# Opening of a two-layer decoder trunk: a first weight unit in two halves, other load orders, another order of TensorE's first steps

## The reference

```python
h = rms_norm(x, norm1_g[l])        # x * rsqrt(mean(x*x) + 1e-6) * g
proj = h @ w_in[l]                 # 1024 -> D_IN columns
...                                # three token mixers, gates, merge
x = x + merged @ w_out[l]
h2 = rms_norm(x, norm2_g[l])
x = x + jnp.square(jax.nn.relu(h2 @ w_ff1[l])) @ w_ff2[l]
```

## Time and profile before

| | us |
|---|---|
| Median of 3 runs (1759.27 to 1759.74) | 1759.31 |
| Span of the profiled execution, first to last instruction | 1757.8 |
| Its own time less its span, taken as median less span | about 1.5 |
| PE busy | 1743.5 (99%) |
| POOL busy | 1067.3 (61%) |
| DVE busy | 957.3 (54%) |
| ACT busy | 690.3 (39%) |

### The profile page before, as it was taken

One profiled execution on the slowest core, in us unless ns is written; L12 is line 12 of the kernel. 1 busy time (PEld: TensorE's weight loads), 2 busy tenths in 40 slices (PEclk: granted clock), 3 DMA queues, 4 the chain that ended last, 5 costly groups with the idle time before them and its releaser, 6 DMA issues.

```text
span 1757.8 us, 26298 instructions
## 1 busy us (share of the span) xinstructions
PE 1743.5 (99%) x10006; PEld 1427.0 (81%) x10006; DVE 957.3 (54%) x1565; ACT 690.3 (39%) x1241; POOL 1067.3 (61%) x572
## 2 busy tenths in 40 slices
PE   8999999999999999999999999999999999999999
PEld 7787888778888888888787888887888888888887
DVE  6796626653442555444566965366443435444445
ACT  6423316550104444444355243176411154444442
POOL 7454466246665777777774535662456657777776
PEclk9999999999999999999999999999999999999999
DMA  6222133133235666666442221331322356666655
GB/s 201 84 73 73 50 96 108 37 98 94 88 101 163 161 173 157 167 168 157 130 156 80 77 62 61 96 96 37 115 89 92 100 153 159 162 173 157 170 153 144
DMA packets 58896, 207.18 MB, mean 118 GB/s; under 512 B 6368, under 2 KB 8704, under 8 KB 58784
## 3 DMA queue, kind: packets, MB, share of 16 engines
q1 hardware_dynamic: 47520, 164.94, 30.0%
q0 software_dynamic: 9216, 33.56, 10.2%
q10 hardware_dynamic: 2048, 7.10, 1.1%
HBM read 184.61 MB, written 4.19 MB: 107 GB/s over the span
## 4 chain that ended last, share of the span: by engine, by line
PE 97%; ACT 1%; DVE 1%; issue 0%; DMA 0%; POOL 0%; SPq 0%; DVEq 0%; ACTq 0%; POOLq 0%
PE ps L666 23%; PE ps L668 22%; PE ps L667 22%; PE ps L1263 6%; PE ps L1265 6%; PE ps L1264 6%; PE ps L1135 2%; PE ps L1144 1%; PE ps L1157 1%; PE ps L685 1%; PE ps L908 1%; PE ps L895 0%; PE ps L945 0%; PE ps L1207 0%; PE ps L931 0%
## 5 line engine op out<-in xcount | busy, mean ns | idle before, releaser
L666 PE MATMUL ps<-hHi,wHi 128*128 128x512 f32 x1360 | 552.9, 407 | 0.0
L668 PE MATMUL ps<-hHi,wLo 128*128 128x512 f32 x1360 | 530.4, 390 | 0.0
L667 PE MATMUL ps<-hLo,wHi 128*128 128x512 f32 x1360 | 529.8, 390 | 0.0
L566 POOL TENSOR_SCALAR wHi<-wraw 128x1024 fp32r<-128x1024 f32 x168 | 181.8, 1082 | 491.6 <-PE ps L668 474.4
L571 POOL TENSOR_TENSOR wLo<-wraw,wHi 128x1024 fp32r<-128x1024 f32 x168 | 415.9, 2476 | 13.8
L597 POOL TENSOR_TENSOR wLo<-w,wHi 128x1024 fp32r<-128x1024 f32 x96 | 239.2, 2514 | 140.5 <-ACT wHi L1694 140.1
L666 PEld LDWEIGHTS ps<-hHi,wHi 128*128 128x128 f32 x1360 | 255.4, 188 | 59.1 <-issue 7.0
L667 PEld LDWEIGHTS ps<-hLo,wHi 128*128 128x128 f32 x1360 | 255.7, 188 | 54.7 <-issue 3.8
L668 PEld LDWEIGHTS ps<-hHi,wLo 128*128 128x128 f32 x1360 | 255.3, 188 | 54.2
L1263 PE MATMUL ps<-wHi,fHi 128*128 128x512 f32 x448 | 174.8, 390 | 1.7 <-issue 1.7
L1265 PE MATMUL ps<-wHi,fLo 128*128 128x512 f32 x448 | 174.4, 389 | 0.0
(11 more groups left out here) (337 smaller groups left out, 2674.7 us busy)
## 6 DMA issues: line engine op xcount, KB each, us to landing
wraw<-stream SPq DMA_DIRECT2D x224, 512.0 KB, 3.5
w<-stream SPq DMA_DIRECT2D x64, 512.0 KB, 4.3
w<-w POOLq DMA_DIRECT2D x32, 512.0 KB, 6.8
b<-stream SPq DMA_DIRECT2D x16, 512.0 KB, 3.5
b<-stream POOLq DMA_DIRECT2D x16, 512.0 KB, 6.1
w<-stream POOLq DMA_DIRECT2D x16, 512.0 KB, 8.1
xin<-x SPq DMA_DIRECT2D x4, 512.0 KB, 6.3
y<-x ACTq DMA_DIRECT2D x1, 2048.0 KB, 10.2
```

The costliest lines, as they stand in the source:

```text
L566: nc.gpsimd.tensor_scalar(wHi[:, slot], wraw[:, slot % RAW], 1.0, 0.0, ALU.mult, ALU.add).then_inc(unit_high, 1)
L666: mm(o, lh[lc], rh[rc], start=start, stop=False)
L667: mm(o, lh[lc], rl[rc], start=False, stop=False)
L668: return mm(o, ll[lc], rh[rc], start=False, stop=stop)
```

## The change

SP's order of loads becomes: x part 0, first half of weight unit 0, x part 1, second half of unit 0, unit 1, x parts 2 and 3, tables. POOL's order becomes: high and low of unit 0's first half, high of its second half, high of unit 1, low of unit 0's second half, low of unit 1. ACT's queue loads the first eight columns of the parameters (norm1's factors) first, then the identity, then the other parameters. PE's hand-written order becomes another, the first pass of a `high_step` waits for `h_high` instead of `h_lo`, and `sum_stream` has all of unit 0 and four low steps of unit 1 ahead of it and four behind it. PE now waits at its start for the identity and the norm factors both. Two pairs of semaphores are made one each (`const_zero` and `tri_done`; `lanes_zero` and `lanes_set`), with their waits at the count that fits.

```diff
             for part in range(4):
-                cols = np.s_[part * 256:(part + 1) * 256]
-                sp.dma_start(xin[:, :, cols], ...).then_inc(x_in[part], 16)
-                if part == 1:
-                    for slot in range(RAW):
-                        load_unit(slot, slot)
+            def load_half(half, loaded):
+                cols = np.s_[half * 512:(half + 1) * 512]
+                sp.dma_start(wraw[:, 0, cols], stream[0][:, cols]).then_inc(loaded, 16)
+            load_x(0)
+            load_half(0, first_loaded)
+            load_x(1)
+            load_half(1, raw_loaded[0])
+            load_unit(1, 1)
+            for part in range(2, 4):
+                load_x(part)
...
-            for slot in range(RAW):
-                high(slot, 1)
-            for slot in range(RAW):
-                low(slot, slot)
+            high_half(0, first_loaded, first_halves)
+            low_half(0, first_halves, FIRST_HIGH, first_halves)
+            high_half(1, raw_loaded[0], unit_high)
+            high(1, 1)
+            low_half(1, unit_high, 1, unit_split)
+            low(1, 1)
...
-            pe.wait_ge(ident_in, 16)
+            pe.wait_ge(ident_in, 32)
...
                 def high_step(slot, k):
-                    pe.wait_ge(unit_high, slot + 1)
-                    pe.wait_ge(h_lo, k + 1)
+                    if slot == 0 and k < KD // 2:
+                        pe.wait_ge(first_halves, FIRST_HIGH)
+                    else:
+                        pe.wait_ge(unit_high, slot + 1)
+                    pe.wait_ge(h_high, k + 1)
                     mm(bank_of(slot), wHi[...], hHi[:, k], ...)
+                    pe.wait_ge(h_lo, k + 1)
                     mm(bank_of(slot), wHi[...], hLo[:, k], ...)
...
                 if layer == 0:
-                    turn_stream(0, range(0, 4))
+                    turn_stream(0, range(0, 2))
                     high_step(0, 0)
+                    turn_stream(0, range(2, 4))
                     high_step(0, 1)
-                    turn_stream(0, range(4, 6))
                     high_step(1, 0)
                     high_step(1, 1)
+                    low_step(0, 0)
+                    low_step(0, 1)
                     high_step(0, 2)
+                    high_step(1, 2)
+                    turn_stream(0, range(4, 6))
+                    high_step(0, 3)
+                    high_step(1, 3)
                     turn_stream(0, range(6, KD))
-                    high_step(1, 2)
-                    for k in range(3, KD):
+                    for k in range(4, KD):
                         high_step(0, k)
                         high_step(1, k)
-                        if k >= 4:
-                            low_step(0, 2 * k - 8)
-                            low_step(0, 2 * k - 7)
+                        if k == 4:
+                            for early in range(2, 4):
+                                low_step(0, early)
+                            for early in range(4):
+                                low_step(1, early)
+                    for k in range(4, KD):
+                        low_step(0, k)
                     sum_stream(0)
-                    for k in range(KD):
+                    for k in range(4, KD):
                         low_step(1, k)
...
+            act.dma_start(prm[:, 0:KD], params[0][:, 0:KD]).then_inc(ident_in, 16)
             act.dma_start(cst[:, 0:P], constants[:, 0:P]).then_inc(ident_in, 16)
-            act.dma_start(prm[:, 0:PRM["bsp"][0]], ...).then_inc(prm_loaded, 16)
+            act.dma_start(prm[:, KD:PRM["bsp"][0]], ...).then_inc(prm_loaded, 16)
```

More of the change, by code:

```diff
@@ L478, in load_unit, with load_x @@
                              ).then_inc(raw_loaded[slot], 16)
-            for part in range(4):
+            def load_x(part):
                 cols = np.s_[part * 256:(part + 1) * 256]
                 sp.dma_start(xin[:, :, cols], x[:, cols].rearrange("(t p) d -> p t d", p=P)).then_inc(x_in[part], 16)
-                if part == 1:
-                    for slot in range(RAW):
-                        load_unit(slot, slot)
+            def load_half(half, loaded):
[8 more added lines that the diff above has]
+                load_x(part)
             sp.dma_start(cst[:, P:], constants[:, P:NCST_F32]).then_inc(tables_in, 16)
@@ L577, in split, with high_half, low_half @@
                 low(slot, done_before)
-            for slot in range(RAW):
-                high(slot, 1)
-            for slot in range(RAW):
-                low(slot, slot)
+            def high_half(half, loaded, done):
+                cols = np.s_[half * 512:(half + 1) * 512]
+                pool.wait_ge(loaded, 16)
+                nc.gpsimd.tensor_scalar(wHi[:, 0, cols], wraw[:, 0, cols], 1.0, 0.0, ALU.mult, ALU.add).then_inc(done, 1)
+            def low_half(half, high_done, count, done):
+                cols = np.s_[half * 512:(half + 1) * 512]
+                pool.wait_ge(high_done, count)
+                nc.gpsimd.tensor_tensor(wLo[:, 0, cols], wraw[:, 0, cols], wHi[:, 0, cols].bitcast(F32), ALU.subtract).then_inc(done, 1)
+            high_half(0, first_loaded, first_halves)
[4 more added lines that the diff above has]
+            low(1, 1)
             for slot in range(RAW, RING):
@@ L730, in high_step @@
                 def high_step(slot, k):
-                    pe.wait_ge(unit_high, slot + 1)
+                    if slot == 0 and k < KD // 2:
[3 more added lines that the diff above has]
+                    pe.wait_ge(h_high, k + 1)
+                    mm(bank_of(slot), wHi[:, slot, k * P:(k + 1) * P], hHi[:, k], start=k == 0, stop=False)
                     pe.wait_ge(h_lo, k + 1)
-                    mm(bank_of(slot), wHi[:, slot, k * P:(k + 1) * P], hHi[:, k], start=k == 0, stop=False)
                     mm(bank_of(slot), wHi[:, slot, k * P:(k + 1) * P], hLo[:, k], start=False, stop=False)
                 def low_step(slot, k):
-                    pe.wait_ge(unit_split, slot + 1)
+                    if slot == 0 and k < KD // 2:
+                        pe.wait_ge(first_halves, FIRST_LOW)
+                    else:
+                        pe.wait_ge(unit_split, slot + 1)
                     last = mm(bank_of(slot), wLo[:, slot, k * P:(k + 1) * P], hHi[:, k], start=False, stop=k == KD - 1)
@@ L1340, in stream_high @@
                 gain = "g2" if norm % 2 else "g1"
-                if norm % 2 == 0:
+                if norm == 0:
+                    act.wait_ge(ident_in, 32)
+                elif norm % 2 == 0:
                     act.wait_ge(prm_loaded, 16 * (norm // 2 + 1))
@@ L1369, in _ @@
             stream_root(0)
+            act.wait_ge(prm_loaded, 16)
             act.wait_ge(tables_in, 48)
-            act.wait_ge(const_zero, 1)
+            act.wait_ge(const_ready, 1)
             act.wait_ge(select_in, 64)
@@ L1800, in stream_low @@
                 gain = "g2" if norm % 2 else "g1"
-                if norm % 2 == 0:
+                if norm == 0:
+                    dve.wait_ge(ident_in, 32)
+                elif norm % 2 == 0:
                     dve.wait_ge(prm_loaded, 16 * (norm // 2 + 1))
```

26 lines of the change are left out of this document (14 added, 12 removed).

## The result

The changed kernel takes 1761.75 us (median of 21 runs, 1760.34 to 1768.47), the kernel before 1759.65 in the same series (21 runs, 1759.24 to 1760.58): ratio 1.0012, interval 1.0006 to 1.0017. It is 2.1 us slower, where 0.6 was forecast, and half a microsecond above the forecast's range. By the bound of 0.2% it is "no change", clear of noise all the same. Two later series of the unaltered kernel gave +1.3 us (its interval just takes in no change) and +1.8 us. Its runs scatter more than those of the kernel before, and the first profiled one is the highest of all, 1768.5 us with a span of 1766.5. I read it as an enlargement of what the others have in little. One run of `before_dve_wait` (6531 us) and one of the kernel before beside `warm_after` (2487 us) lie far off, and the ratios leave them out.

What follows compares the result with a forecast made beforehand. PE, busy 1743.5 of 1757.8 us, was taken to bound the kernel; -0.05 us for the opening and +0.65 for the norm root gave +0.6, so 1759.31 became 1759.9 us, range 1758.7 to 1761.2.

Steps and rivals of the forecast that it cites:

- the bound of 0.2%: Whole kernel: differences under about 0.2%, or 3.5 us, count as no change; chance of landing within it 0.96.
- unit 2: Weight load after the opening: issued at 11.4 instead of 12.6, not on the path, no cost.
- the later waits: Wait for the rest of the parameters behind the norm root: costed at nothing, since they landed long before.
- the row sums are late by what was said: After the opening: with four low steps behind them instead of eight, sums end 0.92 us later relative to PE's work.
- `xrow` behind POOL's subtraction: DVE after the norm root: moved by 0.9 us, an xrow asks at 27.46 and waits for POOL to 29.4.
- 44 passes less 4: Opening after about 10.2 us: passes said to remain, with 16 transposes and the row sums, the same on both sides.
- The opening's term: PE's opening to about 10.2 us: gain of 0.05 us, bounded by a gain of 0.5 and a loss of 0.6.
- the other bound, 6.2: Opening: latest landing of the identity, second on ACT's queue, expected between 4.7 and 6.2 us, taken as 4.8.
- The bound of 0.6 for a loss: Opening: largest loss allowed there, 0.6 us, if the identity lands at 6.2.
- the third rival: Opening: PE's clock rises late, each packed microsecond at the lower level costing half; with the stall 1761.2 us; chance 0.12.
- The term of 0.65 for the norm root: Before q2 at 52 to 53 us: later row sums delay DVE, so PE waits 0.65 us, bounds 0 and 0.9.

Runs made afterwards that it cites:

- before_dve_wait: The kernel before with one added wait: DVE begins the rotation angles only when POOL has copied unit 2; +2.43 us, ratio 1.0014.
- warm_after: The changed kernel with six early matmuls of a zeroed tile on TensorE before its data arrive; +1.63 us against the kernel before, ratio 1.0019.
- pe_ident: The changed kernel with the identity first on ACT's queue and PE waiting for it alone; +1.42 us against the kernel before, ratio 1.0010.
- after_third: The changed kernel, unaltered, in a third series; +1.84 us against the kernel before, ratio 1.0011.
- before_sum_late: The kernel before with four of unit 1's low steps moved ahead of the row sums, nothing else; -0.04 us, ratio 0.9999.
- pe_ident_rot: The changed kernel, identity first and waited for alone by PE, rotation angles moved behind conv(5) and conv(6); +1.05 us against the kernel before, ratio 1.0004.
- rot_late: The changed kernel with the rotation angles moved behind conv(5) and conv(6); +1.06 us against the kernel before, ratio 1.0007.
- warm_rot: The changed kernel with six early zeroed matmuls and the rotation angles behind conv(5) and conv(6); +0.75 us against the kernel before, ratio 1.0005.
- after_again: The changed kernel run again without an edit; +1.28 us against the kernel before, ratio 1.0008.

## Why the prediction was wrong

**What held.** PE bounds the kernel; the opening is all that the change can touch; unit 2, the merged semaphores and the later waits cost nothing; apart from the slower passes of the first trace nothing arises after 60 us. POOL takes the first half at 5.67, the landing forecast was 5.6; the row sums are late by what was said; and `xrow` behind POOL's subtraction is real. Where the working says "44 passes less 4", it should say 48 less 4; the times beside it are right.

**The opening's term failed: a gain of 0.05 us, with the high part of unit 1 "there at 10.1, as before".** It was a loss of 0.35, 0.94 and 1.87 us in three traces. Three steps of it were off. The identity was put at 4.8 "since only 4 KB stands ahead of it"; it landed at 5.8, near the other bound, 6.2, and what that costs by itself is not shown. Unit 1 was "unchanged, 8.8", and POOL began its copy at 9.4 to 9.9; PE waited 0.40 and 0.49 us for it in `pe_ident` and `warm_after`, but in the three traces of the changed kernel PE was later still, and it cost nothing. And "PE ran at half rate, the level of 1.2 GHz, until about 9.4" was carried over as if it were the clock's own time. With the level up early (`warm_after`), PE still starting at 5.8, k1 is at 24.24, against 24.30, 24.89 and 25.82: the late rise is hardly anything of the loss in the first trace and most of it in the two later ones. By the spacing of transposes and passes, in ten traces with the changed loads and no early matmuls it rose between about 9.3 and 12.5, in the four with the order of before and its place for the loads between about 8.5 and 10. PE's work was packed more tightly against that level than before, so each microsecond by which the rise is delayed costs half of one. The bound of 0.6 for a loss did not have it in; the third rival did, "a rise at 12.8 costs 1.3", and `after_third` is that case. It was given 0.12, and the loss there is 1.87. What sets the moment of the rise stays open.

**A step was left out: what DVE does between the last `hLo` and `xrow`.** The prediction said "`rstdT` and DVE's first instruction come at about 25.95", as if DVE had nothing else to do. It found the very mechanism for one instruction at 27.46, and did not ask which others had been moved into POOL's path when transposes 6 and 7 went back by two microseconds. They are eleven, and in the three traces of the changed kernel PE idled between nothing and 5.1 us behind them. `before_dve_wait` shows it alone.

**The term of 0.65 for the norm root was over-sized**: alone it is 0.2 to 0.5 us of idle in two traces (`before_sum_late`, `pe_ident_rot`), none in two others (`rot_late`, `warm_rot`), and nothing that the medians show. So it was luck that the sum had the right sign: the term that made it positive is the one that the medians do not show, and what made the kernel slower was put at a gain or left out.

The rule that the prediction cited, the Trainium skill, "SBUF — State Buffer", section "SBUF: two separate sides", agrees with the traces, but not in the breadth in which the prediction gave it. The section names only some VectorE instructions, and here too the second `lowrow` instruction, one element for each partition, took its 0.14 us in the middle of POOL's subtraction of 19.52 to 21.92. Applied to the whole stretch it would have pointed at the collisions; of the opening it says nothing.

## What to carry to other kernels

When a step is moved, list everything that its successors do on each engine until the next thing on the critical path, and lay it beside the other engines' timelines of that stretch; small instructions count by where they fall, not by their length. Work that is brought forward into a time when TensorE is still at its lower clock level is brought forward at half value. A load put second on a queue to let a smaller one go first may lose more than the smaller one gains.

## What the runs showed of the hardware

- A DVE instruction on 4 elements for each partition takes 0.17 us alone and up to 2.2 us beside POOL's subtraction; it ends within 0.03 us of the end of POOL's. An instruction with a PSUM source (`convd`, 0.75) keeps its time beside the same POOL work, and so do those on one element for each partition (`lowrow`, 0.14).
- Six matmuls on zeros between 2.0 and 4.7 us had the clock at its upper level by about 7 us in four executions and not in a fifth (`warm_rot`, about 9.9). The level seems to follow more than the amount of work ahead of it. The Trainium skill, "TensorE: Matmul & The Clock Gate", Part 1, says that the moment of the rise varies from run to run, by 0.5 us to either side. The traces agree that it varies, but by more: in the three of the unaltered changed kernel it rose at about 9.5, 10.5 and 12.4. What else decides it was not tried.
- After 4.5 us without work PE fell back to 1.2 GHz, and in `before_dve_wait` it was there after waits of 1.3 and 1.0 us with short matmuls between; after a single wait of 0.94 us in `after_again` it was not. By the two windows of the first trace it was there for (1 - 0.84) x 2 x 8.5 + (1 - 0.90) x 2 x 20 = 6.7 us, over 5 of them with passes back to back.
- The second load on ACT's queue landed 4.5 to 5.3 us after its issue, be it 4, 64 or 71 KB, while the first took 3.1 to 3.8.
